# Second and final norms of a transformer block on Trainium2: square roots and reciprocals taken with tokens on partitions and spread back by a ones x diagonal matmul, with the end of the last token tile written in another order

## The reference

```python
def rms_norm(x, g):
    y = xf * lax.rsqrt(jnp.mean(xf * xf, axis=-1, keepdims=True) + EPS)
    return (y * g.astype(jnp.float32)).astype(x.dtype)
...
    x = x + ga1 * (merged @ w_out[l])
    h = rms_norm(x, g_ffn[l]) * (1 + sc2) + sh2          # the second norm
    gu = h @ w_ffn_in[l]
    g_part, u_part = jnp.split(gu, 2, axis=-1)
    x = x + ga2 * ((jax.nn.silu(g_part) * u_part) @ w_ffn_out[l])
return rms_norm(x, g_final)                              # the final norm
```

## Time and profile before

| | |
|---|---|
| median of 3 runs | 1040.62 us (1040.14 to 1040.85) |
| profiled execution: device time of the slowest core | 1040.1 us |
| its span (first to last instruction, core 6, the slowest) | 1038.4 us |
| spans of the eight cores | 1033.8 to 1038.4 us |
| PE busy on core 6 | 956.9 us (92%) |
| DVE, ACT, POOL busy on core 6 | 575.9, 390.7, 208.3 us |

### The profile page before, as it was taken

How to read it: one execution, slowest core, us unless ns; L and a number is a source line. 1 busy time by engine, 2 the same in 40 slices (tenths; PEclk the granted TensorE clock), 3 DMA queues, 4 the chain that set the end, 5 groups by cost and what they waited for, 6 DMA issues and landing times.

```text
span 1038.4 us, 15386 instructions; the slowest of 8 cores (1033.8 to 1038.4 us)
## 1 busy us (share of the span) xinstructions
PE 956.9 (92%) x5475; PEld 450.4 (43%) x5571; DVE 575.9 (55%) x819; ACT 390.7 (38%) x600; POOL 208.3 (20%) x282
## 2 busy tenths in 40 slices
PE   0499999999999999999989999999999999999993
PEld 0444444444444444444434444444444444444443
DVE  0427858685868786868876512244212243253656
ACT  3467545454545454545357611100111100234233
POOL 3000222132221211113554210000100001113213
PEclk9799999999999999999989999999999999999997
DMA  9970563676363533123702352200622203120222
GB/s 213 185 202 1 79 106 43 103 103 82 52 119 98 131 103 51 18 44 53 121 11 31 52 81 41 34 8 1 92 41 41 41 1 45 27 82 1 82 82 82
DMA packets 44650, 72.25 MB, mean 70 GB/s; under 512 B 19600, under 2 KB 21904, under 8 KB 42528
## 3 DMA queue, kind: packets, MB, share of 16 engines
q0 software_dynamic: 21600, 45.36, 28.7%
q1 hardware_dynamic: 22976, 25.91, 8.2%
HBM read 108.15 MB, written 8.45 MB: 112 GB/s over the span
## 4 chain that ended last, share of the span: by engine, by line
PE 77%; DVE 10%; issue 4%; DMA 4%; ACT 3%; POOL 1%; DVEq 0%; ACTq 0%; POOLq 0%
PE psum L964 29%; PE psum L584 25%; PE psum L977 14%; PE psum L906 5%; DVE rden L761 4%; DMA wadaB<-w_ada_l 4%; PE psum L736 2%; PE psum L712 1%; DVE cv L659 1%; DVE nrm L762 1%; DVE pT L724 1%; PE psum L468 1%; DVE cv L667 1%; DVE h L527 1%; DVE u L647 1%
## 5 line engine op out<-in xcount | busy, mean ns | idle before, releaser
L584 PE MATMUL psum<-h,ws 128*128 128x512 bf16 (+1 forms) x1695 | 360.7, 363 | 12.3 <-issue 5.7
L964 PE MATMUL psum<-h,fws 128*128 128x512 bf16 x1379 | 305.4, 380 | 1.5
L584 PEld LDWEIGHTS psum<-h,ws 128*128 128x128 bf16 x1744 | 160.3, 98 | 182.2 <-issue 30.6
L964 PEld LDWEIGHTS psum<-h,fws 128*128 128x128 bf16 x1408 | 138.2, 98 | 169.0 <-issue 5.1
L972 DVE TENSOR_TENSOR mg<-psum,sg 128x512 bf16<-128x512 f32 x88 | 60.7, 690 | 198.6 <-PE psum L964 193.5
L969 ACT ACTIVATE sg<-psum 128x512 bf16<-128x512 f32 x88 | 52.4, 597 | 308.6 <-PE psum L964 300.0
L977 PE MATMUL psum<-mg,fwo 128*128 128x512 bf16 (+1 forms) x747 | 152.4, 363 | 1.7 <-DVE mg L972 1.0
L761 DVE RECIPROCAL rden<-rden 128x256 f32<-128x256 f32 x64 | 111.9, 1749 | 13.9 <-ACT rden L759 13.1
L984 DVE SCALAR_TENSOR_TENSOR xres<-psum,modc,xres 128x512 f32<-128x512 f32 (+1 forms) x104 | 73.8, 710 | 78.2 <-PE psum L977 77.5
L775 POOL TENSOR_TENSOR mg<-nrm,cv 128x256 bf16<-128x256 f32 x64 | 54.0, 844 | 304.2 <-DVE nrm L764 156.7
L977 PEld LDWEIGHTS psum<-mg,fwo 128*128 128x128 bf16 x760 | 74.3, 98 | 79.2 <-issue 1.5
(11 more groups left out here) (89 smaller groups left out, 691.4 us busy)
## 6 DMA issues: line engine op xcount, KB each, us to landing
ws<-w_in_l POOLq DMA_DIRECT2D x50, 256.0 KB, 5.8
fws<-w_fi_l POOLq DMA_DIRECT2D x44, 256.0 KB, 4.9
wadaB<-w_ada_l POOLq DMA_DIRECT2D x20, 512.0 KB, 7.6
xres<-xtok SPq DMA_DIRECT2D x8, 1024.0 KB, 11.0
xres<-xt SPq DMA_DIRECT2D x8, 1024.0 KB, 6.1
out<-xres SPq DMA_DIRECT2D x12, 512.0 KB, 3.0
fwo<-w_fo_l POOLq DMA_DIRECT2D x22, 256.0 KB, 6.7
wadaA<-w_ada_l POOLq DMA_DIRECT2D x4, 512.0 KB, 23.0
```

Of the source, the lines that this page charges most:

```text
L584: P.op("pe", [lambda e, k=k: e.matmul(bank(b)[:, 0:n], lhsT=WS[s * 1024 + k * 128, s * 1024 + (k + 1) * 128], rhs=hk(k, col, n), start=(k ...
L964: P.op("pe", [lambda e, k=k, w=w, wo=wo, b=b: e.matmul(bank(b), lhsT=w[wo + k * 128, wo + (k + 1) * 128], rhs=hk(k, 128 + tt * 512, 512), ...
```

## The change

`rstd_of` no longer works on [128 x n] tiles. For each block of 128 tokens a float32 matmul takes the 128 x 128 piece of `ACC` as weights and one column of ones as the moving operand, so the total of token p lands in row p of one PSUM column: four such matmuls for 512 tokens, two for 256. The root (ACT) and the reciprocal (DVE) then work on [128 x 4] or [128 x 2]. To bring the values back onto all partitions, DVE multiplies the bfloat16 identity `IDENT` with the reciprocals, broadcast, into a float32 tile [128 x n] of diagonal blocks, and PE multiplies it by `ONESF` in one float32 matmul into the same PSUM bank. All users read that bank.

The last tile changes in five ways. The last `ff_in` splits its Silu and its product into two halves of 256 tokens. A square root of one element is recorded behind the last Silu. Of the first half's squares DVE adds two, where it added none; of the second half's DVE added five and now adds one (chunk 5), and the squares of chunks 6 and 7 aren't added but enter the column matmuls by themselves (`more`). The first half's norm is issued behind chunk 4 of the second half. In the first half DVE scales chunks 0 and 1 instead of 6 and 7, and POOL reads a copy of the spread values that ACT makes.

```diff
-        def rstd_of(total, n, sd, slack, b, in_psum):
-            P.op("pe", [lambda e: e.matmul(bank(b)[:, 0:n], lhsT=ONESF.t[:], rhs=total[0][total[1], total[1] + n], start=True, stop=True)],
-                 reads=[ONESF.iv(), total[0].iv(total[1], total[1] + n)], writes=[pv_(b)], cost=4 * n / 2400 + 0.2, lat=slack)
+        def rstd_of(srcs, n, sd, slack, b):
+            nk = n // 128
             d, o = sd
-            P.op("act", lambda e: e.activation(out=d[o, o + n], in_=bank(b)[:, 0:n], func=AF.Sqrt, bias=EPSC.t[:], scale=1.0 / D),
-                 reads=[pv_(b), EPSC.iv()], writes=[d.iv(o, o + n)], cost=act_us(n))
-            P.op("dve", lambda e: e.reciprocal(out=bank(b)[:, 0:n] if in_psum else d[o + n, o + 2 * n], in_=d[o, o + n]),
-                 reads=[d.iv(o, o + n)], writes=[pv_(b)] if in_psum else [d.iv(o + n, o + 2 * n)], cost=0.1 + n * 0.0066)
+            last = len(srcs) - 1
+            for m, (t, a) in enumerate(srcs):
+                P.op("pe", [lambda e, m=m, t=t, a=a, i=i: e.matmul(bank(b)[:, i:i + 1], lhsT=t[a + i * 128, a + (i + 1) * 128],
+                                                                   rhs=ONESF.t[:, 0:1], start=(m == 0 and i == 0),
+                                                                   stop=(m == last and i == nk - 1), skip_group_check=True) for i in range(nk)],
+                     reads=[ONESF.iv(), t.iv(a, a + n)], writes=[pv_(b)], cost=0.25 * nk, lat=slack)
+            P.op("act", lambda e: e.activation(out=d[o, o + nk], in_=bank(b)[:, 0:nk], func=AF.Sqrt, bias=EPSC.t[:], scale=1.0 / D),
+                 reads=[pv_(b), EPSC.iv()], writes=[d.iv(o, o + nk)], cost=0.3)
+            P.op("dve", lambda e: e.reciprocal(out=d[o + 8, o + 8 + nk], in_=d[o, o + nk]),
+                 reads=[d.iv(o, o + nk)], writes=[d.iv(o + 8, o + 8 + nk)], cost=0.16)
+            P.op("dve", lambda e: e.tensor_tensor(out=d[o + 512, o + 512 + n].rearrange("p (i t) -> p i t", i=nk),
+                                                  in0=IDENT.t[:].rearrange("p (o t) -> p o t", o=1).to_broadcast([128, nk, 128]),
+                                                  in1=d[o + 8, o + 8 + nk].rearrange("p (i o) -> p i o", o=1).to_broadcast([128, nk, 128]),
+                                                  op=ALU.mult),
+                 reads=[IDENT.iv(), d.iv(o + 8, o + 8 + nk)], writes=[d.iv(o + 512, o + 512 + n)], cost=0.1 + n / 900)
+            P.op("pe", [lambda e: e.matmul(bank(b)[:, 0:n], lhsT=ONESF.t[:], rhs=d[o + 512, o + 512 + n], start=True, stop=True)],
+                 reads=[ONESF.iv(), d.iv(o + 512, o + 512 + n)], writes=[pv_(b)], cost=4 * n / 2400 + 0.1)
...
+            if n < 512 and len(on_dve) < 8:
+                P.op("act", lambda e: e.activation(out=RS[ro + 768, ro + 768 + n], in_=bank(sb)[:, 0:n], func=AF.Copy),
+                     reads=[pv_(sb)], writes=[RS.iv(ro + 768, ro + 768 + n)], cost=act_us(n))
...
-                    ff_in(j, js.index(j), tt)
+                    ff_in(j, js.index(j), tt, (0, 256, 512) if tt == 3 and j == js[-1] else (0, 512))
...
-            out_of(3, 3, 0, 256, every, False)
-            out_of(4, 3, 256, 256, every, True)
-            finish_tile(3, 0, 256, 3, (6, 7))
-            finish_tile(3, 256, 256, 4, every)
+            P.op("act", lambda e: e.activation(out=RS[512, 513], in_=EPSC.t[:], func=AF.Sqrt), reads=[EPSC.iv()], writes=[RS.iv(512, 513)],
+                 cost=1.5, after=(P.last["act"],))
+            out_of(3, 3, 0, 256, every, ("pool",) * 6 + ("dve",) * 2)
+            how = ("pool",) * 5 + ("dve", None, None)
+            out_of(4, 3, 256, 256, every[:5], how)
+            finish_tile(3, 0, 256, 3, (0, 1))
+            more = out_of(4, 3, 256, 256, every[5:], how)
+            finish_tile(3, 256, 256, 4, every, more)
```

More of the change, by code:

```diff
@@ L968, in ff_in @@
             sgn[0] += 1
-            P.op("act", lambda e: e.activation(out=SG[o, o + 512], in_=bank(bs[0]), func=AF.Silu),
-                 reads=[pv_(bs[0])], writes=[SG.iv(o, o + 512)], cost=act_us(512, 0))
-            m0 = jl * 2048 + tt * 512
-            P.op("dve", lambda e: e.tensor_tensor(out=MG[m0, m0 + 512], in0=bank(bs[1]), in1=SG[o, o + 512], op=ALU.mult),
-                 reads=[pv_(bs[1]), SG.iv(o, o + 512)], writes=[MG.iv(m0, m0 + 512)], cost=dve_us(512, 1, True))
+            for c0, c1 in zip(cuts, cuts[1:]):
+                n = c1 - c0
+                m0 = jl * 2048 + tt * 512 + c0
+                P.op("act", lambda e, c0=c0, c1=c1: e.activation(out=SG[o + c0, o + c1], in_=bank(bs[0])[:, c0:c1], func=AF.Silu),
+                     reads=[pv_(bs[0])], writes=[SG.iv(o + c0, o + c1)], cost=act_us(n, 0))
+                P.op("dve", lambda e, c0=c0, c1=c1, m0=m0, n=n: e.tensor_tensor(out=MG[m0, m0 + n], in0=bank(bs[1])[:, c0:c1], in1=SG[o + c0, o + c1],
+                                                                               op=ALU.mult),
+                     reads=[pv_(bs[1]), SG.iv(o + c0, o + c1)], writes=[MG.iv(m0, m0 + n)], cost=dve_us(n, 1, True))
         def ff_out(nj, tt, co, lo, n):
@@ L993, in finish_tile @@
             sb = 6 + i % 2
-            on_bank = len(on_dve) == 8 or n == 512
-            rstd_of((ACC, (i % 2) * 512), n, (RS, ro), 1.5 if n == 512 else 0.0, sb, on_bank)
+            rstd_of([(ACC, (i % 2) * 512)] + list(more), n, (RS, ro), 1.5 if n == 512 else 0.0, sb)
+            if n < 512 and len(on_dve) < 8:
+                P.op("act", lambda e: e.activation(out=RS[ro + 768, ro + 768 + n], in_=bank(sb)[:, 0:n], func=AF.Copy),
+                     reads=[pv_(sb)], writes=[RS.iv(ro + 768, ro + 768 + n)], cost=act_us(n))
             P.prio = pos[0] + (14 if n == 512 else 1)
@@ L998, in finish_tile @@
                 a0, a1 = xi(tt, co, lo, n)
-                rs = bank(sb)[:, 0:n] if on_bank else RS[ro + n, ro + 2 * n]
-                io = dict(reads=[X.iv(a0, a1), pv_(sb) if on_bank else RS.iv(ro + n, ro + 2 * n), cst_iv], writes=[X.iv(a0, a1)])
+                rs = bank(sb)[:, 0:n]
+                io = dict(reads=[X.iv(a0, a1), pv_(sb), cst_iv] + ([RS.iv(ro + 768, ro + 768 + n)] if n < 512 and len(on_dve) < 8 else []),
+                          writes=[X.iv(a0, a1)])
                 if n == 512 or co in on_dve:
                     P.op("dve", lambda e, co=co, a0=a0, a1=a1: e.scalar_tensor_tensor(
-                            out=X[a0, a1], in0=X[a0, a1], scalar=cst(O_GFIN + co), in1=rs, op0=ALU.mult, op1=ALU.mult), cost=dve_us(n), **io)
+                            out=X[a0, a1], in0=X[a0, a1], scalar=cst(O_GFIN + co), in1=rs, op0=ALU.mult, op1=ALU.mult), cost=dve_us(n, 1, True), **io)
                 else:
@@ L1006, in finish_tile @@
                          reads=[X.iv(a0, a1), cst_iv], writes=[X.iv(a0, a1)], cost=act_us(n), prio=P.prio - 8)
-                    P.op("pool", lambda e, a0=a0, a1=a1: e.tensor_tensor(out=X[a0, a1], in0=X[a0, a1], in1=rs, op=ALU.mult),
-                         cost=pool_us(n), **io)
+                    P.op("pool", lambda e, a0=a0, a1=a1: e.tensor_tensor(out=X[a0, a1], in0=X[a0, a1], in1=RS[ro + 768, ro + 768 + n], op=ALU.mult),
+                         reads=[X.iv(a0, a1), RS.iv(ro + 768, ro + 768 + n)], writes=[X.iv(a0, a1)], cost=pool_us(n))
                 if co % 2 == 1:
@@ L1047, in build_program, with out_of @@
                 load_fo(jl, j)
-            def out_of(i, tt, lo, n, cos, end):
+            def out_of(i, tt, lo, n, cos, ends=("pool",) * 8):
+                more = []
                 for co in cos:
@@ L1052, in out_of @@
                     if last:
-                        square_add(tt, co, lo, n, (i % 2) * 512, "pool" if not end or co in (1, 2) else "dve")
+                        r = square_add(tt, co, lo, n, (i % 2) * 512, ends[co])
+                        if r:
+                            more.append(r)
                 if last and n == 512:
                     finish_tile(tt, lo, n, i)
+                return more
             def in_of(tt, part):
@@ L1064, in build_program @@
                 for tt in range(4):
-                    out_of(tt, tt, 0, 512, every, False)
+                    out_of(tt, tt, 0, 512, every)
                 continue
```

10 lines of the change are left out of this document (6 added, 4 removed).

## The result

The changed kernel takes 1045.85 us (median of five runs, 1045.46 to 1046.30), against 1040.16 (1040.06 to 1040.85) for the kernel before on the same chip: ratio 1.0053, 95% interval 1.0043 to 1.0064. It is slower, by 5.7 us; 1045.3 was predicted. In some executions, whatever the kernel, the cores of one die show a lower granted clock and take longer, and every device time of this document is the median of the executions without that.

A forecast was written before the change was run, and what follows sets the result against it. PE was taken as the bound in the feed-forward layer. Terms +5.6 + 7.6 - 0.3 - 3.9 = +9.0 per core, less the stall's part, made the slowest core +4.7: 1044.8, against the median 1045.3 us; range 1040.4 to 1050.0.

The forecast's parts named there:

- term 1: Second norms: PE's stall behind DVE's long reciprocal goes, gaining 6.0 us on core 6, 4.4 on core 0, 1.9 on core 4.
- term 2: Seven norms of 512 tokens: four float32 column matmuls cost PE 0.8 us a norm, +5.6 on every core (0.8 to 10.6).
- The bound below: Column matmuls: lowest price, from the trace's bfloat16 row of 32 matmuls in 0.99 us, 0.12 a norm.
- term 3: Norms of 512 tokens: PE waits at spreading matmuls, five times 1.3 us and 1.1 at the third second norm, +7.6.
- chain of seven steps: Final norms, from columns through table load, root, reciprocal and identity product back to PE: 3.04 us against 1.73 of PE work.
- term 4: Last tile: its first product starts earlier, half a product taking 0.43 us instead of 0.69, -0.3.
- term 5: Last tile: first output matmul to end of last scaling takes 20.6 us instead of 24.5, -3.9.
- Transfers still follow the last scaling as before: Program end: output transfers come behind the last scaling as in the kernel before; no size of its own.
- The cheap columns: Rival: float32 column weights load as fast as bfloat16, costing 0.8 us instead of 5.6; 1040.5, no change; chance 0.13.
- the table load that runs ahead: Rival: ACT loads the root's table while awaiting the columns, so the new waits vanish; 1037.7, faster; chance 0.07.
- the clock that falls at the new waits: Rival: PE's granted clock falls at some of six new waits, 2 us each at three, +6; 1051; chance 0.12.

The follow-up runs named there:

- short reciprocal: Kernel before, with the reciprocal of the second of the four second norms on 4 columns instead of 512: 1036.6 us, ratio 0.9955.
- far spread: Changed kernel, planner's cost of the small root raised from 0.3 to 1.9 us, putting spreading matmuls 16 or 24 matmuls behind the columns: 1038.7 us.
- double columns: Changed kernel, with the one-column float32 matmuls of the seven norms of 512 tokens issued twice (doubled groups): 1052.8 us, ratio 1.0107.
- tail only: Changed kernel, with the seven norms of 512 tokens in the old form and only the last tile's end changed: 1037.4 us, ratio 0.9961.

## Why the prediction was right

The sum came out as its steps did; one step was right in size for a wrong reason.

*The stall (term 1): right.* 6.0, 4.4 and 1.9 us were stated for cores 6, 0 and 4; the short reciprocal measured 6.0, 4.6 and 2.0. It didn't come back.

*Columns (term 2): right.* 0.8 a norm was read off two float32 loads 0.11 apart, less what hides; it is 0.81, 5.7 in all, and the doubled groups show the 0.11 a pass (0.89 for eight more). The bound below, the bfloat16 row, is what bfloat16 weights do cost here (0.11 a norm), so the choice between the two rows was the whole question.

*New waits (term 3): right in sum.* 7.6 predicted, 7.6 measured (five of 1.27, one of 1.21), and none at the second of the second norms. What the term left out is that a spreading matmul behind a wait isn't as cheap as the old one: 0.94 instead of 0.86, 0.5 at six places, so that the far spread gave back 8.05. The product with the identity took the 0.69 that was taken from another operation of its shape, except where POOL was in an addition; that cost PE 0.77 once, on core 6. In the final norms the chain of seven steps is shown as stated, and the table load as its largest. In the first and the fourth of the second norms ACT's own work ends just when the columns do, which the prediction had said of the third only.

*Half product (term 4): right*, 0.75 idle instead of 1.01.

*The end (term 5): the step "Transfers still follow the last scaling as before" failed.* The predicted -3.9 was for the last scaling's end, which came 2.1 earlier on core 1, and the program's end came 3.4 earlier. The end hangs on POOL's last scaling, which it follows by 8.32 us, and neither on DVE's last scaling nor on the transfers. POOL's scalings end 35.69 - 17.38 = 18.3 us behind the first output matmul, where 18.4 was predicted and 21.7 was measured before: this is the 3.4, and the prediction had it among its steps without taking it for the end. That the gain was right to half a microsecond is luck: a last scaling that was 1.8 us later than predicted would have made it 2.1 if the program's end had followed it. The last scaling itself was late by 1.8 on core 1 for two reasons. DVE's accumulation of chunk 5 waited for POOL and then took 0.99 instead of the usual 0.41, since it began just behind the start of a POOL scaling, so the last square is there at 15.7, not 14.8. And the last spreading matmul ran at half clock (1.19), which the text had put at +0.9 and left out of the sum.

*Sum.* For core 4, by the table: +11.34 in the middle (11.0 predicted), -3.4 at the end (-3.9), +7.9 in all against +7.1. The slowest core was predicted at 1043.1 with a first norm at 523.58; in the execution after, core 1 had its first norm at 523.67 and a span of 1044.0. So the sum was 0.8 us short, and in device time +4.7 was predicted and +5.7 measured. The two medians are closer than that, 1045.3 and 1045.85, only because the forecast was built on 1040.6 for the kernel before, which took 1040.16 this time.

*Rivals.* The cheap columns are refuted by 0.81; the table load that runs ahead by the idle 1.90 us that it ended (it does run ahead when an instruction asks for it); the clock that falls at the new waits by the 1.00 of the windows.

## What to carry to other kernels

A wait on the engine that bounds the kernel can be worth several microseconds of it while the cure is on another engine: reorder or split the one late instruction there (here a 3.36 us reciprocal in front of seven additions) before giving the bounding engine more to do. When a computation is sent back through the bounding engine's in-order list, count the whole chain between leaving it and coming back, table loads included, and put that much work in between: here eight to sixteen matmuls more between the two were worth 8 us. And when the end of a kernel is moved, look at what closes the program, and not at the last instruction that works: here the end moved with POOL's last instruction, 3.4 us earlier in the changed kernel and 0.7 later with seven scalings. How far it could still be moved isn't shown; the last transfer landed 1.6 us before POOL's DRAIN was over.

## What was unexpected of the hardware

A DVE instruction with two inputs in SBUF waited for the POOL addition that was running. In the seven kernels with the new form for norms of 512 tokens there are 344 products with the identity on 128x512. 279 began when POOL was in none of its additions, and all took 0.69 us. The other 65 began inside one, and took what was left of it and 0.55 more: 0.91 was left at 525.74 on core 6 of the changed kernel, and the product took 1.46; 0.53 was left at 527.37 on core 0 of the double columns, and it took 1.08. Only where less than 0.14 was left was it 0.69 again. The POOL addition that followed took 1.5 instead of 1.27. At the end of the program an addition of 128x256 in float32 on DVE, 0.41 us alone, took 0.99 when it began just behind the start of one of POOL's scalings. The Trainium skill ("Trainium Architecture — The Big Picture", What this means for kernel authors) says that the port pair that DVE and GpSimd share is taken as an exclusive lock; these rows agree with that.

The program ended 8.32 us behind the last instruction of POOL's list, 8.09 of them in POOL's closing DRAIN, on all 96 cores traced, where DVE's took 0.05.

In the kernel before, an idle stretch of about 3 us was followed by a fallen clock on cores 0, 3, 6 and 7 (middles of 484.6 to 486.5), and on cores 1, 2 and 5 it was not (483.5). It isn't the core: in the trace of the tail only, with the same stretch of 2.7 to 3.0 us, the clock fell on cores 0, 1, 3, 4 and 6 (0.92 in the window 538 to 560) and stayed at 1.00 on 2, 5 and 7. What decides it was not found.
